# Conditioning weights in tiles of 1024 columns, one step a tile, placed behind consecutive weight units

## The chip, the cores and the metric

One core of one Trainium2 chip runs the whole layer. The metric is the device time in microseconds (us) of one execution; lower is better. The kernel before takes 1895.23 us (median of 3 runs, 1892.63 to 1897.20).

## The reference

One layer of a streaming-encoder trunk on 256 frames of width 2048, all in f32: a SwiGLU branch (hidden width 5632), a mixer branch (multi-head latent attention beside a forgetting attention) and a second SwiGLU branch. Each branch is modulated by vectors that come from the conditioning row `c`:

```
cond = silu(c)                                  # (1, 2048)
mod  = cond @ w_ada + b_ada                     # w_ada is 2048 x 18432
sh1, sc1, gt1, sh2, sc2, gt2, sh3, sc3, gt3 = split(mod, 9)
h = modulate(rmsnorm(x, g_pre), sh, sc)         # h * (1 + sc) + sh
y = rmsnorm(swiglu(h, w_gate, w_up, w_down), g_post)
x = x + 0.5 * gt * y                            # the mixer: x + gt2 * rmsnorm(mixer(h))
```

The change concerns only how `cond @ w_ada` is computed beside the large products. That product is one row by 151 MB of weights.

## The kernel before, in words

**The large products.** All weights stream through the core once. A weight unit ("W") is 256 rows by 512 columns, 512 KB, one DMA into a slot of `raw`. ScalarE rounds it to fp32r (`w_hi`, L566), VectorE takes the difference (`w_lo`, L925), and TensorE makes 12 products of it (L1459 to L1461: hi by hi, hi by lo, lo by hi, two row chunks, two frame tiles). In four blocks of the projection stage `win` (n = 2 to 5) the weights stand as the loaded operand and a unit is 24 products of 256 columns (L1508 to L1511).

**The conditioning product.** It doesn't go to TensorE but to VectorE: a tile ("A") of `w_ada` is multiplied by a column of `silu(c)` and added to `acc` (`ada_unit`). A tile holds, on each partition, 2 rows of 512 columns (512 KB), so it takes two dependent steps (L944) with a drain ahead of each. Eight tiles make a "quarter" of 512 columns; then a transpose (L950) and a reduction (L953) put the sums over 32 partitions into `part_sum`, and later TensorE finishes the sum over partitions (`sum_columns`, L1616) and VectorE adds the bias (`mod_columns`). The first 64 tiles' worth is done at the start by another path (`start_ada`, L965, steps of 1024 columns), which the change leaves alone.

**The order of the work.** It is written out in `make_plan`. Blocks follow each other: `pre` and `gu1` (gate and up of the first SwiGLU, 16 W a block, the first four blocks opened together), `down1` (4 blocks of 22 W), `win` (8 blocks of 8 W), `uq`, `ukv`, attention, `wo` (4 blocks of 8 W), `gu2`, `down2`. `pattern(n_w, ada_after)` says behind which W of a block an A stands. The same order holds on SP's queue (the DMAs), on ScalarE and on VectorE. 32 KB of each partition are a ring of 8 slots (`RING`) shared by W and A; `w_lo` is written over the W's own slot, and `w_hi` has 4 buffers (`HI_RING`). A load waits until the tile 8 places ahead of it in the order is done with: a W when TensorE has finished it (`w_used`), an A when VectorE has (`raw_used`). SP issues strictly in order.

VectorE also has work at fixed places of a block: in `gu` blocks `hidden` before W4 (L1103) and `lo_hid` before W7 (L1109), in `down` blocks the eviction of the block before at W4 (L1120), in `win` blocks many small ones (`before_unit`). Four groups of conditioning columns have to be complete at set places, the ends of `GROUPS`: quarters 12, 20, 24, 32 and 36. `RUNS` says which blocks run as a hardware loop.

Of the kernel before, what the change touches and what calls it, by code (L numbers as in the profile page):

```python
# [93 lines left out]
class Block:  # L94
# [17 lines left out]
    def r_of(self, u):  # L112
        return self.r + self.seq.index(("W", u))

    def quarter(self, u):
        return (self.a + u) // 8, (self.a + u) % 8


def make_plan():
    at = dict(r=0, w=0, a=0, g=0)  # L120
    pl = {}


    pl["pre"] = [Block(at, woven(WOVEN.count("W") * "W"), 3 * OPEN)]
    at["a"] += 2 * KD * DB // 2
    gu_ada = pattern(16, [4, 5, 7, 8, 10, 11, 13, 14])
    gu = pattern(16, [])

    gu_ada0 = pattern(16, list(range(8, 16)))
    pl["gu1"] = [Block(at, woven(text), 2) for text in ("WWAWAW", "WWAWAW", "WWAWWA", "WWAWAW")]  # L130
    pl["gu1"] += [Block(at, gu_ada, 2) for b in range(OPEN_FF, FB - 4)]
    gu_more = [u for u in range(16) if u % 4 != 3]
    pl["gu1"] += [Block(at, pattern(16, gu_more), 2) for b in range(4)]

    pl["down1"] = [Block(at, pattern(22, [u for u in range(2, 21) if u % 6 != 4] if n < DB - 1 else list(range(0, 16, 2))), 1) for n in range(DB)]
    win_ada = [[6, 7], [3, 5, 7], [1, 3, 5, 6, 7]] + 5 * [[1, 3, 4, 5, 6, 7]]
    pl["win"] = [Block(at, pattern(8, after), 1) for after in win_ada]
    pl["uq"] = [Block(at, pattern(2, []), 1) for _ in range(3)]
    pl["ukv"] = [Block(at, pattern(1, []), 1) for _ in range(4)]
    pl["wo"] = [Block(at, pattern(8, after), 1)  # L140
                for after in ([1, 2, 3, 4], [1, 3, 4, 5, 6, 7], [1, 3, 4, 5, 6, 7], [])]
    pl["gu2"] = [Block(at, gu_ada0 if b == 0 else gu_ada if b < 4 else gu, 2) for b in range(FB)]
    pl["down2"] = [Block(at, pattern(22, []), 1) for _ in range(DB)]
    assert at["a"] == 8 * N_MOD * DB
    order = [kind for blocks in sorted(pl.values(), key=lambda v: v[0].r) for b in blocks for kind, _ in b.seq]
    assert len(order) == at["r"]


    tp, owner = {}, []

    def fills(name, n, by):
        tp[name] = len(owner)
        owner.extend((by * n)[:n])

    for f in ("1", "2"):

        fills("mod" + f, 8 if f == "1" else 4, "a" if f == "1" else "va")
        fills("hid" + f, 2 * (FB - 1), "v")
        fills("gate" + f, 4, "a")
        fills("hidlast" + f, 2, "v")  # L160
        if f == "1":
            fills("modmix", 4, "va")
            fills("qa", 2, "v")
            fills("kv", 1, "v")
            fills("kpe", 1, "v")
            fills("qr", 2, "v")
            fills("pt", 2 * HEADS, "a")
            fills("gatemix", 4, "a")
    taken = [(o, owner[:n + 1].count(o)) for n, o in enumerate(owner)]
    return pl, tp, taken, order  # L170


def build(nc, A, const, out):
    pl, tp, taken, order = make_plan()
    ctx = ExitStack()
    with ctx:
# [22 lines left out]
        x = sb("x", [P, TT, D])  # L199
        y = sb("y", [P, TT, D])  # L200
        s = sb("s", [P, TT, NB])
        acc = sb("acc", [P, 2, NB])
        tmp = sb("tmp", [P, 2, NB])

        h_hi = sb("h_hi", [P, KD, SEQ], F32R)
# [2 lines left out]
        with ExitStack() as mix:  # L208
            def mx(name, shape, dt=F32):
                return mix.enter_context(nc.sbuf_tensor(name, shape, dt))  # L210
            qa_hi = mx("qa_hi", [P, Q_RANK // P, SEQ], F32R)
            qa_lo = mx("qa_lo", [P, Q_RANK // P, SEQ], F32R)
            ka_hi = mx("ka_hi", [P, KV_RANK // P, SEQ], F32R)
            ka_lo = mx("ka_lo", [P, KV_RANK // P, SEQ], F32R)
            fqk = mx("fqk", [P, 2 * HEADS, SEQ])
            fv = mx("fv", [P, TT, HEADS * P])
            v_mla = mx("v_mla", [P, TT, HEADS * DV])
            qnT = mx("qnT", [P, HEADS, SEQ])
            knT = mx("knT", [P, HEADS, SEQ])

            qrT = mx("qrT", [P, HEADS // 2, SEQ])
            krT = mx("krT", [P, 2, SEQ])
            sel = mx("sel", [P, HEADS, P])
            sel_b = mx("sel_b", [P, HEADS, P], BF16)
            lf = mx("lf", [P, TT, P])

            cumT = mx("cumT", [P, SEQ], BF16)
# [19 lines left out]
        newton = sb("newton", [P, TT])  # L247
        warm = sb("warm", [P, 1])
        rstd = sb("rstd", [P, TT])
        kpe = sb("kpe", [P, 2, TT, 2 * ROPE])  # L250
        forget = sb("forget", [P, KD, HEADS])
        fz = sb("fz", [P, 5, TT, HEADS])
        nbias = sb("nbias", [P, 2, TT])
# [110 lines left out]
        GATE = {"ffn1": 0, "mix": 1, "ffn2": 2}  # L364
        N_ATT = 2 * HEADS

        RUNS = {"gu1": ((OPEN_FF, FB - 4 - OPEN_FF), (FB - 4, 1), (FB - 3, 1), (FB - 2, 1), (FB - 1, 1)), "gu2": ((1, 1), (2, 2), (4, 1), (5, FB - 5))}

        def start_weight(w):

# [45 lines left out]

        @block.sync
        def _(sp):
            ada = A["w_ada"].rearrange("(p j) n -> p j n", j=KD)

            def load(r, src, n=NB, i=0, per=0, per_w=0):

# [6 lines left out]
                        sp.wait_ge(raw_used, plus(before + 1, i, per))  # L429
                sp.dma_start(raw[:, r % RING, :, 0:n], src).then_inc(raw_landed[r % RING], 16)  # L430

            def stream(b, unit, i=0, per=0, per_w=0, per_q=0):

                for n, (kind, u) in enumerate(b.seq):
                    if kind == "W":
                        src, cols = unit(u)
                        load(b.r + n, src, cols, i, per, per_w)
                    else:
                        q, j = b.quarter(u)
                        c0, j = plus(q, i, per_q) * NB, 2 * j  # L440
                        load(b.r + n, ada[:, j:j + 2, bass.ds(c0, NB)], NB, i, per, per_w)

            def unit_of(w, cols, at):
                v = w.rearrange("(k p) n -> p k n", p=P)
# [40 lines left out]
            for f, gu, down in (("1", "gu1", "down1"), ("2", "gu2", "down2")):  # L485
# [6 lines left out]
                for start, count in RUNS[gu]:  # L492
                    b = pl[gu][start]
                    if count == 1:
                        stream(b, gate_up(wg, wu, start))
                        continue
                    with sp.Fori(0, count) as i:
                        stream(b, gate_up(wg, wu, i + start), i, len(b.seq), 16, int(b.na > 0))
                for n, b in enumerate(pl[down]):
                    stream(b, unit_of(wd, NB, n * NB))  # L500
                if f == "2":
# [415 lines left out]
        def _(dve):  # L917
# [7 lines left out]
                nc.vector.tensor_tensor(w_lo[:, r % RING, :, 0:n], raw[:, r % RING, :, 0:n],  # L925
                                        w_hi[:, w % HI_RING, :, 0:n], ALU.subtract).then_inc(raw_used, 1)

            def ada_unit(b, n, a, i=0, per=0):


                r, (q, j0) = b.r + n, b.quarter(a)
                if j0:
                    dve.drain()  # L933
                dve.wait_ge(raw_landed[r % RING], landed(r, i, per))
                for k in range(2):
                    j = 2 * j0 + k
                    into = acc[:, 0, :]
                    if k:
                        dve.drain()
                    if j == 0:  # L940
                        ins = nc.vector.tensor_scalar(into, raw[:, r % RING, k, :], c_col[:, 1, j:j + 1],
                                                      None, ALU.mult)
                    else:
                        ins = nc.vector.scalar_tensor_tensor(into, raw[:, r % RING, k, :], c_col[:, 1, j:j + 1],  # L944
                                                             into, ALU.mult, ALU.add)
                ins.then_inc(raw_used, 1)
                if j0 == 7:
                    first, _, base = next(g for g in GROUPS if g[0] <= q < g[1])
                    dve.drain()
                    nc.vector.transpose(acc[:, 1, :], acc[:, 0, :])  # L950
                    dve.drain()
                    at = bass.ds(plus((base + q - first) * 4 * DB, i, 4 * DB if per else 0), 4 * DB)
                    nc.vector.tensor_reduce(part_sum[:, at], acc[:, 1, :].rearrange("p (b j) -> p b j", j=32), AX_X,  # L953
                                            ALU.add).then_inc(part_ready, 1)

            def start_ada(n):

# [10 lines left out]
            def run(b, tasks=None, i=0, per=0, per_w=0, start=0, stop=None, n=NB, before=None):  # L968
# [3 lines left out]
                for at in range(a, z):  # L972
                    kind, u = b.seq[at]
                    if kind == "A":
                        ada_unit(b, at, u, i, per)
                        continue
                    if before is not None:
                        before(u)
# [238 lines left out]
            for f, gu, down in (("1", "gu1", "down1"), ("2", "gu2", "down2")):  # L1217
# [29 lines left out]
                for n, b in enumerate(pl[down]):  # L1247
                    def last_down(n=n):
                        if n:
                            evac_y(pl[down][n - 1], k_y, n - 1, gate_ffn, fills[n - 1])  # L1250

                    def sums(n=n):
                        mod_columns(n // 2 + 1)
                    run(b, {4: last_down, 16: sums} if f == "1" and n in (1, 3) else {4: last_down}, start=2 if n == 0 else 0)
                if f == "2":
                    branch_end(pl[down][-1], k_y, gate_ffn, fills[-1])
                    break
# [192 lines left out]
        def _(pe):  # L1450
# [232 lines left out]
            for f, gu, down in (("1", "gu1", "down1"), ("2", "gu2", "down2")):  # L1683
# [25 lines left out]
                for n, b in enumerate(pl[down]):  # L1709
                    bank_free(b.g)  # L1710
                    for u in range(18 if n == DB - 1 else 22):
                        if n == 0 and u == 20:
                            pe.wait_ge(t_taken[who], count)
                        if f == "1" and n in (1, 3) and u == 6:
                            sum_columns(n // 2 + 1)
                        unit(b, u, hid_hi, hid_lo, 2 * u, b.g, u == 0, u == 21)
                    if n == DB - 1:
                        skewed_units(b, hid_hi, hid_lo, lambda u: 2 * u)
                if f == "2":
# [208 lines left out]
```

## Time and profile before

| | us |
|---|---|
| median of 3 runs | 1895.23 |
| lowest and highest | 1892.63, 1897.20 |
| the profiled execution, its own time | 1891.84 |
| its span, first to last instruction | 1890.1 |
| TensorE busy in it | 1850.8 (98%) |
| VectorE busy | 1359.9 (72%) |
| ScalarE busy | 895.2 (47%) |

The granted TensorE clock was 0.998 over the span. A busy time counts from the start of an instruction to its modelled end, and the products of TensorE overlap: two starts in a row are closer together than one product is long.

### The profile page before, as it was taken

The page shows a single profiled execution, that of the slowest core. Times are in us where ns is not written, and L with a number is a line of the kernel's source. Part 1 is how long each engine was busy: PE and PEld are TensorE (multiplying, and loading weights), DVE is VectorE, ACT ScalarE, POOL GpSimd, SP SyncE. Part 2 cuts the span into 40 slices and gives each one's busy share as a digit, 9 for nine tenths or more (in the row PEclk, how much of TensorE's full clock was granted, in tenths as well). Part 3 has the DMA queues.
Part 4 walks back from the last instruction along what each step waited for, and adds up shares of the span by engine and source line. Part 5 has one row for each costly group of instructions (what it writes and reads, how often), then busy time and mean ns, then how long its engine had stood idle before and what let it go on. Part 6 is the DMA issues. An engine that isn't in the chain of part 4 may idle for free.

```text
span 1890.1 us, 24649 instructions
## 1 busy us (share of the span) xinstructions
PE 1850.8 (98%) x9016; PEld 1557.5 (82%) x9016; DVE 1359.9 (72%) x1618; ACT 895.2 (47%) x1145; POOL 0.2 (0%) x4
## 2 busy tenths in 40 slices
PE   6999999999999999999999999999999999999998
PEld 6888888888888878899988788888888888888886
DVE  5998877889888888789786778878445445444444
ACT  4677644444444434654446446444444444434443
POOL 0000000000000000000000000000000000000000
PEclk9999999999999999999999999999999999999999
DMA  9998788999989998578992685888666666555553
GB/s 374 407 399 275 238 278 286 322 326 332 325 291 331 333 317 305 180 257 277 322 311 69 208 282 180 307 288 282 211 189 189 189 189 188 178 191 195 194 192 131
DMA packets 265052, 488.47 MB, mean 258 GB/s; under 512 B 21638, under 2 KB 32252, under 8 KB 264700
## 3 DMA queue, kind: packets, MB, share of 16 engines
q1 hardware_dynamic: 264080, 486.67, 76.7%
q8 instruction: 59, 0.97, 0.2%
q10 hardware_dynamic: 876, 0.53, 0.1%
q14 instruction: 37, 0.30, 0.1%
HBM read 485.04 MB, written 2.10 MB: 258 GB/s over the span
## 4 chain that ended last, share of the span: by engine, by line
PE 81%; DVE 8%; DMA 5%; DVEq 3%; ACT 2%; issue 1%; ACTq 0%; SPq 0%
PE pair L1459 25%; PE pair L1461 25%; PE pair L1460 25%; DVE acc L944 2%; DVE w_lo L925 2%; PE tps L1542 2%; DMA raw<-in_w_down 1%; DVEq L933 1%; DVE start_acc L965 1%; DMA raw<-in_w_in 1%; DMA start_raw<-in_w_ada 1%; ACT w_hi L566 1%; DVEq L964 1%; DMA raw<-in_w_up 1%; DMA raw<-in_w_gate 1%
## 5 line engine op out<-in xcount | busy, mean ns | idle before, releaser
L566 ACT ACTIVATE w_hi<-raw 128x1024 fp32r<-128x1024 f32 x634 | 667.9, 1056 | 883.1 <-PE pair L1461 417.4
L925 DVE TENSOR_TENSOR w_lo<-raw,w_hi 128x1024 fp32r<-128x1024 f32 x634 | 767.7, 1217 | 385.2 <-ACT w_hi L566 382.9
L1459 PE MATMUL pair<-w_hi,h_hi 128*128 128x512 f32 (+1 forms) x1656 | 645.8, 390 | 4.2 <-DVE w_lo L925 2.9
L1461 PE MATMUL pair<-w_hi,h_lo 128*128 128x512 f32 (+1 forms) x1656 | 642.3, 388 | 0.0
L1460 PE MATMUL pair<-w_lo,h_hi 128*128 128x512 f32 (+1 forms) x1656 | 641.9, 388 | 0.0
L1459 PEld LDWEIGHTS pair<-w_hi,h_hi 128*128 128x128 f32 x1656 | 310.9, 188 | 68.2 <-issue 2.9
L1461 PEld LDWEIGHTS pair<-w_hi,h_lo 128*128 128x128 f32 x1656 | 310.9, 188 | 63.9
L1460 PEld LDWEIGHTS pair<-w_lo,h_hi 128*128 128x128 f32 x1656 | 311.0, 188 | 61.9
L944 DVE SCALAR_TENSOR_TENSOR acc<-raw,c_col,acc 128x512 f32<-128x512 f32 x420 | 315.7, 752 | 47.8 <-DMA raw<-in_w_ada 12.7
L1459 PE MATMUL pair<-w_hi,hid_hi 128*128 128x512 f32 x704 | 275.6, 391 | 1.3 <-DVE w_lo L925 1.2
L1461 PE MATMUL pair<-w_hi,hid_lo 128*128 128x512 f32 x704 | 274.1, 389 | 0.0
L1460 PE MATMUL pair<-w_lo,hid_hi 128*128 128x512 f32 x704 | 274.0, 389 | 0.0
L1459 PEld LDWEIGHTS pair<-w_hi,hid_hi 128*128 128x128 f32 x704 | 132.1, 188 | 32.8 <-DVE w_lo L925 5.8
L1461 PEld LDWEIGHTS pair<-w_hi,hid_lo 128*128 128x128 f32 x704 | 132.1, 188 | 27.7
L1460 PEld LDWEIGHTS pair<-w_lo,hid_hi 128*128 128x128 f32 x704 | 132.2, 188 | 26.9
L965 DVE SCALAR_TENSOR_TENSOR start_acc<-start_raw,c_col,start_acc 128x1024 f32<-128x1024 f32 x55 | 70.7, 1285 | 14.7 <-DMA start_raw<-in_w_ada 9.7
L1508 PE MATMUL pair<-h_hi,w_hi 128*128 128x256 f32 x256 | 73.1, 286 | 4.5 <-DVE w_lo L925 4.5
L1510 PE MATMUL pair<-h_lo,w_hi 128*128 128x256 f32 x256 | 72.4, 283 | 0.0
L1511 PE MATMUL pair<-h_hi,w_lo 128*128 128x256 f32 x256 | 72.4, 283 | 0.0
L1508 PEld LDWEIGHTS pair<-h_hi,w_hi 128*128 128x128 f32 x256 | 49.1, 192 | 5.5 <-DVE w_lo L925 2.9
L1510 PEld LDWEIGHTS pair<-h_lo,w_hi 128*128 128x128 f32 x256 | 49.1, 192 | 0.0
L1511 PEld LDWEIGHTS pair<-h_hi,w_lo 128*128 128x128 f32 x256 | 49.1, 192 | 0.0
(211 smaller groups left out, 872.9 us busy)
## 6 DMA issues: line engine op xcount, KB each, us to landing
raw<-in_w_ada SPq DMA_DIRECT2D x224, 512.0 KB, 4.6
raw<-in_w_gate SPq DMA_DIRECT2D x176, 512.0 KB, 4.3
raw<-in_w_up SPq DMA_DIRECT2D x176, 512.0 KB, 4.0
raw<-in_w_down SPq DMA_DIRECT2D x176, 512.0 KB, 4.0
start_raw<-in_w_ada SPq DMA_DIRECT2D x64, 512.0 KB, 9.4
raw<-in_w_in SPq DMA_DIRECT2D x56, 512.0 KB, 4.8
raw<-in_w_o SPq DMA_DIRECT2D x32, 512.0 KB, 4.7
raw<-in_w_uq SPq DMA_DIRECT2D x12, 256.0 KB, 4.3
```

The lines of the kernel that those rows point to most:

```text
L566: nc.scalar.activation(w_hi[:, w % HI_RING, :, 0:n], raw[:, r % RING, :, 0:n], ACT.Copy).then_inc(hi_ready, 1)
L925: nc.vector.tensor_tensor(w_lo[:, r % RING, :, 0:n], raw[:, r % RING, :, 0:n], w_hi[:, w % HI_RING, :, 0:n], ALU.subtract).then_inc(raw_us ...
L933: dve.drain()
L944: ins = nc.vector.scalar_tensor_tensor(into, raw[:, r % RING, k, :], c_col[:, 1, j:j + 1], into, ALU.mult, ALU.add)
L965: ins = nc.vector.scalar_tensor_tensor(total, tile, c_col[:, 1, j:j + 1], total, ALU.mult, ALU.add)
L1459: nc.tensor.matmul(o, hi, wh, start=first and kk == 0, stop=False, skip_group_check=added)
L1460: nc.tensor.matmul(o, hi, wl, start=False, stop=False, skip_group_check=added)
L1461: ins = nc.tensor.matmul(o, lo, wh, start=False, stop=last and kk == 1, skip_group_check=added)
L1508: nc.tensor.matmul(o, wh, hi, start=first and kk == 0 and c % 2 == 0, stop=False, skip_group_check=True)
L1510: nc.tensor.matmul(o, wh, lo, start=False, stop=False, skip_group_check=True)
L1511: ins = nc.tensor.matmul(o, wl, hi, start=False, stop=last and kk == 1, skip_group_check=True)
L1542: ins = nc.tensor.transpose(tps[0:rows, n % 2, k * P:(k + 1) * P], src, ident)
```

## The change

What it does:

- An A tile now holds, on each partition, one row of 1024 columns (two quarters, a "half"), and takes one step; 16 tiles make a half. `acc` has three parts: two for the sums and one for the transpose.
- At the end of a half the first quarter is transposed and reduced at once (`row_sums`), the second ahead of the first step of the next half, or at once too where a group ends there (after quarters 11, 19, 23, 31, 35).
- The number of A tiles (224 here) and of W units in each block stays; their places change in `gu1` blocks 7 to 10 (12 A, behind u = 4 to 15, before behind each u with u % 4 != 3) and in `down1` (16 A behind u = 4 to 19, before behind 16 of u = 2 to 20; in the last block 8 A behind u = 4 to 11, before behind every second u).
- Blocks with A tiles no longer run as loops (`RUNS`): `gu1` 4 to 6 and `gu2` 2 and 3 are written out.
- `sum_columns` and `mod_columns` in `down1` stand at the end of blocks 0 and 2, and behind the eviction in blocks 1 and 3.
- `kpe` lies in another part of the memory.

```diff
-    def quarter(self, u):
-        return (self.a + u) // 8, (self.a + u) % 8
+    def half(self, u):
+
+        return divmod(self.a + u, KD)
...
-    gu_more = [u for u in range(16) if u % 4 != 3]
+    gu_more = [4, 5, 6, 7, 8, 9, 10, 11, 12, 13, 14, 15]
...
-    pl["down1"] = [Block(at, pattern(22, [u for u in range(2, 21) if u % 6 != 4] if n < DB - 1 else list(range(0, 16, 2))), 1) for n in range(DB)]
+    pl["down1"] = [Block(at, pattern(22, list(range(4, 20 if n < DB - 1 else 12))), 1) for n in range(DB)]
...
-        RUNS = {"gu1": ((OPEN_FF, FB - 4 - OPEN_FF), (FB - 4, 1), (FB - 3, 1), (FB - 2, 1), (FB - 1, 1)), "gu2": ((1, 1), (2, 2), (4, 1), (5, FB - 5))}
+        RUNS = {"gu1": [(b, 1) for b in range(OPEN_FF, FB)], "gu2": [(b, 1) for b in range(1, 5)] + [(5, FB - 5)]}
...
-            ada = A["w_ada"].rearrange("(p j) n -> p j n", j=KD)
+            ada = A["w_ada"].rearrange("(p j) (q n) -> p j q n", j=KD, n=NB)
...
-                        q, j = b.quarter(u)
-                        c0, j = plus(q, i, per_q) * NB, 2 * j
-                        load(b.r + n, ada[:, j:j + 2, bass.ds(c0, NB)], NB, i, per, per_w)
+                        half, j = b.half(u)
+                        load(b.r + n, ada[:, j, 2 * half:2 * half + 2, :])
...
+            def ada_unit(b, n, a):
+
+                r, (half, j) = b.r + n, b.half(a)
+                dve.wait_ge(raw_landed[r % RING], landed(r))
+                into = acc[:, 0:2, :]
+                if j == 0:
+                    if not any(2 * half == first for first, _, _ in GROUPS):
+                        row_sums(2 * half - 1)
+                    ins = nc.vector.tensor_scalar(into, raw[:, r % RING], c_col[:, 1, 0:1], None, ALU.mult)
+                else:
                     dve.drain()
...
+                    ins = nc.vector.scalar_tensor_tensor(into, raw[:, r % RING], c_col[:, 1, j:j + 1], into,
+                                                         ALU.mult, ALU.add)
                 ins.then_inc(raw_used, 1)
...
+                if j == KD - 1:
+                    row_sums(2 * half)
+                    if any(2 * half + 2 == end for _, end, _ in GROUPS):
+                        row_sums(2 * half + 1)
+
+            def row_sums(q):
+
+                first, _, base = next(g for g in GROUPS if g[0] <= q < g[1])
+                at = 4 * DB * (base + q - first)
+                dve.drain()
+                nc.vector.transpose(acc[:, 2, :], acc[:, q % 2, :])
+                dve.drain()
+                nc.vector.tensor_reduce(part_sum[:, at:at + 4 * DB], acc[:, 2, :].rearrange("p (b j) -> p b j", j=32),
+                                        AX_X, ALU.add).then_inc(part_ready, 1)
...
-                        if f == "1" and n in (1, 3) and u == 6:
-                            sum_columns(n // 2 + 1)
                         unit(b, u, hid_hi, hid_lo, 2 * u, b.g, u == 0, u == 21)
+                    if f == "1" and n in (0, 2):
+                        sum_columns(n // 2 + 1)
```

## Rows read from the trace of the kernel before

**Rows 1.** The page, part 1: busy us, share of the span, instructions.
```profile
PE 1850.8 (98%) x9016; PEld 1557.5 (82%) x9016; DVE 1359.9 (72%) x1618; ACT 895.2 (47%) x1145; POOL 0.2 (0%) x4
```
**Rows 2.** The chain of waits, 560 to 724 and at 740: start, length, what.
```profile
571.82 5.92 DMA raw<-in_w_down
...
616.20 0.82 PE mps L1616 x8
...
680.28 6.27 DMA raw<-in_w_down
...
740.00 0.80 PE mps L1616 x8
```
**Rows 3.** Timeline of TensorE at four stalls: start, length, idle before and its releaser.
```profile
216.14 1.09 PE L1542 MATMUL tps<-cst,s 128*128 128x128 f32 x8 [1.13 <-DVE s L1103]
...
688.95 0.50 PE L1459 MATMUL pair<-w_hi,hid_hi 128*128 128x512 f32 x1 [0.30 <-DVE w_lo L925]
689.28 0.39 PE L1460 MATMUL pair<-w_lo,hid_hi 128*128 128x512 f32 x1
...
856.27 0.39 PE L1508 MATMUL pair<-h_hi,w_hi 128*128 128x256 f32 x1 [1.30 <-DVE w_lo L925]
...
1193.36 0.47 PE L1459 MATMUL pair<-w_hi,h_hi 128*128 128x512 f32 x1 [0.69 <-DVE w_lo L925]
```
**Rows 4.** TensorE's waits, 800 to 978: us in total, times, longest.
```profile
PE pair L1508 <- DVE w_lo L925: 4.5, 5, 1.3
PE pair L1459 <- DVE w_lo L925: 0.9, 1, 0.9
```
**Rows 5.** VectorE's groups over the span: busy us, mean ns of one.
```profile
L944 DVE SCALAR_TENSOR_TENSOR acc<-raw,c_col,acc 128x512 f32<-128x512 f32 x420 | 315.7, 752 | 47.8 <-DMA raw<-in_w_ada 12.7 <-issue 3.4
L965 DVE SCALAR_TENSOR_TENSOR start_acc<-start_raw,c_col,start_acc 128x1024 f32<-128x1024 f32 x55 | 70.7, 1285 | 14.7 <-DMA start_raw<-in_w_ada 9.7 <-issue 0.5
L962 DVE TENSOR_SCALAR start_acc<-start_raw,c_col 128x1024 f32<-128x1024 f32 x4 | 3.0, 749 | 5.1 <-ACT c_col L717 5.1
```
**Rows 6.** Timeline of VectorE, 943 to 951, a stretch without idle time.
```profile
943.40 1.57 DVE L944 SCALAR_TENSOR_TENSOR acc<-raw,c_col,acc 128x512 f32<-128x512 f32 x2
944.89 1.22 DVE L925 TENSOR_TENSOR w_lo<-raw,w_hi 128x1024 fp32r<-128x1024 f32 x1
946.20 1.57 DVE L944 SCALAR_TENSOR_TENSOR acc<-raw,c_col,acc 128x512 f32<-128x512 f32 x2
947.87 0.71 DVE L950 STREAM_TRANSPOSE acc<-acc 128x512 f32<-128x512 f32 x1
948.65 0.69 DVE L953 TENSOR_REDUCE part_sum<-acc 128x16 f32<-128x512 f32 x1
949.26 1.22 DVE L925 TENSOR_TENSOR w_lo<-raw,w_hi 128x1024 fp32r<-128x1024 f32 x1
```
**Rows 7.** SP's queue, 1173 to 1185: the DMAs of `gu2` block 0's last units.
```profile
1173.66 0.37 SPq L430 DMA_DIRECT2D raw<-in_w_up  x1
1174.07 0.47 SPq L430 DMA_DIRECT2D raw<-in_w_ada  x1
1176.38 0.37 SPq L430 DMA_DIRECT2D raw<-in_w_up  x1
...
1184.54 5.81 SPq L430 DMA_DIRECT2D raw<-in_w_gate  x5
```
**Rows 8.** ScalarE in the same stretch: start, length, idle before and its releaser.
```profile
1177.34 1.06 ACT L566 ACTIVATE w_hi<-raw 128x1024 fp32r<-128x1024 f32 x1 [1.94 <-DMA raw<-in_w_up]
...
1190.18 1.06 ACT L566 ACTIVATE w_hi<-raw 128x1024 fp32r<-128x1024 f32 x1 [3.26 <-DMA raw<-in_w_gate]
```
**Rows 9.** DMA, median us from issue to landing, 541:724, then 1400:1600.
```profile
raw<-in_w_down SPq DMA_DIRECT2D x65, 512.0 KB, 6.2
...
raw<-in_w_gate SPq DMA_DIRECT2D x39, 512.0 KB, 3.6
```
**Rows 10.** Window 95 to 140: PE, PEld, DVE, ACT, POOL busy us (instructions), PEclk, DMA share, GB/s.
```profile
95.00:140.00 45.00, 45.00 (x208) 37.48 (x207) 41.08 (x39) 36.16 (x54) 0.00 (x0) 1.00 1.05 400
```

More of the change, by code:

```diff
@@ L201, in build @@
         s = sb("s", [P, TT, NB])
-        acc = sb("acc", [P, 2, NB])
+        acc = sb("acc", [P, 3, NB])
         tmp = sb("tmp", [P, 2, NB])
@@ L223, in build @@
             sel = mx("sel", [P, HEADS, P])
+            kpe = mx("kpe", [P, 2, TT, 2 * ROPE])
             sel_b = mx("sel_b", [P, HEADS, P], BF16)
@@ L249, in build @@
         rstd = sb("rstd", [P, TT])
-        kpe = sb("kpe", [P, 2, TT, 2 * ROPE])
         forget = sb("forget", [P, KD, HEADS])
@@ L430, in load, with stream @@
                 sp.dma_start(raw[:, r % RING, :, 0:n], src).then_inc(raw_landed[r % RING], 16)
-            def stream(b, unit, i=0, per=0, per_w=0, per_q=0):
+            def stream(b, unit, i=0, per=0, per_w=0):
                 for n, (kind, u) in enumerate(b.seq):
@@ L497, in _ @@
                     with sp.Fori(0, count) as i:
-                        stream(b, gate_up(wg, wu, i + start), i, len(b.seq), 16, int(b.na > 0))
+                        stream(b, gate_up(wg, wu, i + start), i, len(b.seq), 16)
                 for n, b in enumerate(pl[down]):
@@ L926, in lo_unit @@
                                         w_hi[:, w % HI_RING, :, 0:n], ALU.subtract).then_inc(raw_used, 1)
-            def ada_unit(b, n, a, i=0, per=0):
-                r, (q, j0) = b.r + n, b.quarter(a)
-                if j0:
-                    dve.drain()
[L934 to L945, printed above, removed]
-                ins.then_inc(raw_used, 1)
[L947 to L954, printed above, removed]
@@ L974, in run @@
                     if kind == "A":
[L975 removed]
+                        ada_unit(b, at, u)
                         continue
@@ L1250, in last_down @@
                             evac_y(pl[down][n - 1], k_y, n - 1, gate_ffn, fills[n - 1])
-                    def sums(n=n):
-                        mod_columns(n // 2 + 1)
-                    run(b, {4: last_down, 16: sums} if f == "1" and n in (1, 3) else {4: last_down}, start=2 if n == 0 else 0)
+                            if f == "1" and n in (1, 3):
+                                mod_columns(n // 2 + 1)
+                    run(b, {4: last_down}, start=2 if n == 0 else 0)
                 if f == "2":
```

## The prediction

> **What bounds the kernel now.** The page's busy times come first: TensorE is busy 1850.8 of 1890.1 us [rows 1], so nothing the change does to VectorE or the DMAs can pay except where TensorE waits for them. TensorE's pitch is read off SP's queue: weight loads that wait for a finished unit are issued at 1173.66 and 1176.38, so a unit takes 2.72 us [rows 7]. I then looked for what lies between units in TensorE's waits, its timeline and the chain of waits. The waits that conditioning work has a hand in are these:
>
> - the end of the opening: TensorE waits 1.13 us for `s`, which VectorE makes after an A tile and a transpose and reduction [rows 3].
> - `win`: six waits for `w_lo`, 4.5 + 0.9 = 5.4 us [rows 4], the longest 1.30 at 856.27 [rows 3]. After a wait TensorE doesn't resume at pitch: at 688.95 the next product starts 0.33 us later [rows 3], where 12 products in 2.72 us are 0.23 apart, and more such starts follow. I put this at 0.3 us a wait, so `win` loses 5.4 + 6 x 0.3 = 7.2 us.
> - `down1`: the small sums stand at the same place (ahead of unit 6) of blocks 1 and 3, at 616.20 and 740.00 [rows 2]. Between them are 44 units (119.7 us) and one sum (0.8), but 123.8 us pass: 3.3 us are lost. Block 0 has one more such chain at 571.82 [rows 2]; with it I take 4.3 us.
> - the first unit of `gu2` block 1: 0.69 us at 1193.36 [rows 3], with its slow restart 1.0.
> - about 0.4 in `gu1` block 10 (estimate).
>
> With 1.13 + 0.6 for the opening that is 14.6 us in all: more than that the change cannot gain. The chain of waits names two kinds of cause. In `win` it is VectorE, in `down1` it is "DMA raw<-in_w_down" of 5.92 and 6.27 us, then ScalarE, then VectorE [rows 2].
>
> **What a tile costs VectorE.** From 943.40 to 946.20 one A tile and one weight unit take 2.80 us [rows 6], more than TensorE's 2.72, so VectorE falls behind wherever they alternate. A 512-column step is 0.752 us, a 1024-column one 1.285 [rows 5]; two steps stand as 1.57 to 1.58 [rows 6]. After the change the pair takes 2.80 - 1.58 + 1.285 = 2.51 us: VectorE gains 0.29 us a tile and is again faster than TensorE. The first tile of a half takes 0.749 [rows 5]. A transpose with its reduction delays the next unit from 1.49 after the step's start (943.40 to 944.89) to 3.06 (946.20 to 949.26), so it costs 1.57 [rows 6]; call it RS. There are 28 as before, but they now come in twos: both at once where a group ends, else one behind the sixteenth tile and one ahead of the next.
>
> **The slack of a weight load.** This is the part that speaks against the change. Where W and A strictly alternate, the 8 slots hold 4 W and 4 A, so the load of unit w waits until TensorE has finished unit w-4, and must be landed, rounded and subtracted in 3 x 2.72 = 8.16 us. ScalarE takes 1.06 [rows 8], VectorE 1.22 [rows 6], handing over some 0.1. So a load that takes L us to land is ready 5.78 - L ahead of TensorE, less 0.35 that I allow for TensorE's early weight loading (estimate). Where three A stand to four W, the slot eight places back mostly lies one unit earlier, and 2.72 us are added; the A tile is then issued ahead of the W, which costs the W about 0.9. The change gives up 1.85 us of slack in `gu1` 7 to 10 and in `down1`.
>
> What L is: 3.6 without A tiles, 6.2 as a median in `down1` [rows 9]. `gu2` block 0 already has eight strictly alternating tiles. Its W at 1173.66 is with ScalarE at 1177.34, so L = 3.66; the W at 1184.54, after eight pairs, at 1190.18, so L = 5.62 [rows 7, 8]. An alternating stretch asks for 1.049 MB in 2.72 us = 385 GB/s; the most that a long stretch shows is 400 [rows 10]. So a delay once made goes back by some 0.1 us a pair only.
>
> The Trainium skill's page "DMA: Bandwidth & Descriptors", section "Latency and other measured facts", puts the latency of the memory at 0.2 us on average and 2 us under high load. By it, L would rise by 1.8 to 5.46 throughout an alternating stretch. The 5.62 agrees, the 3.66 three tiles into the same stretch doesn't.
>
> **The sum.** Gains first.
>
> - Opening: RS is no longer behind that tile (the half ends eight tiles later) and two steps are shorter, 1.57 + 0.6 = 2.2 ahead of a wait of 1.13. It goes: -1.7.
> - `win`, with 40 tiles. Two of the RS just ahead of a wait (of quarters 26 and 28, at the end of block 3 and in block 6) move away; with 0.29 for each of the 5 to 6 tiles since VectorE last idled, the waits in block 3, at the start of block 4 and in block 6 go. Block 2 keeps its RS and gets the next one straight behind it: +1.57 - 0.29 x 3 - 0.57 leaves it as it is, 2.4. The wait at 909.32 is a slow DMA's; I keep 0.7 for it. 7.2 becomes 3.1: -4.1.
> - `gu2` block 1: RS between the last tile and W0 goes: -1.0.
>
> Then what alternation costs.
>
> - RS inside an alternating stretch. VectorE has 2.72 - 2.51 = 0.2 spare, so with one RS the next unit is ready 5.78 - 1.4 - L ahead, with two 2.93 - L. With the 0.35 the stall is L - 4.1 and L - 2.6. For `down1` I take L = 5.0, between 3.66 and 6.2 and nearer its own stage. Blocks 0 and 2 end their stretch with two RS: 2 x 2.4. Block 1 with one: 0.9. `gu1` block 9 has one behind W11 and one behind W12: 1.2. `wo` block 3 has one more ahead of W0, partly beside the small sum: 0.4. Together +7.3. What is queued behind an RS is every later `w_lo`; TensorE is who waits.
> - Loads that come late by themselves, W8 to W19 of three blocks in `down1`, 36 units. `gu2` block 0 shows 0 a unit, the waits of `down1` about 0.2 where a load had only this slack. I take 0.12, since a stall itself lets the DMAs catch up: +4.3. `gu1` 7 to 10, 35 units at 0.05: +1.8. Last block of `down1`: +0.2.
> - The old waits of `down1` and `gu1` 10 are replaced by these: -4.7.
>
> Net: -1.7 - 4.1 - 1.0 + 7.3 + 4.3 + 1.8 + 0.2 - 4.7 = +2.1 us.
>
> Costed at nothing: the small sums moved (same 0.8 us on TensorE each, their inputs ready, since the units behind the last A tile are behind it on VectorE too); `kpe`; the written-out loops (no wait stands at the loops' ends, and VectorE is several us ahead there; if code came late it would show as TensorE waiting for "issue"); SP issues the same number of DMAs. Whether rows of 4 KB move faster than two of 2 KB no row shows. They are 128 pieces in place of 256; for a half of the traffic I bound it by -0.1 us a tile and 0, and take 0.
>
> The profiled execution took 1891.84, 3.4 under the median. Made against its own time the sum gives 1893.9; on the median, 1895.2 + 2.1 = 1897.3.
>
> **The rivals.**
>
> A. *VectorE's relief wins.* The DMAs keep up in alternating stretches as in the first seven pairs of `gu2` block 0, L near 4.0. Then the RS cost 2 x 1.4 + 0.2 + 0.3 and late loads 1.0, together 4.3. Gains and old waits are 1.7 + 4.1 + 1.0 + 4.7 = 11.5, so the sum is -7.2: 1888. For it: VectorE is under TensorE's pitch everywhere, fewer and longer pieces, W ahead of A in each pair. Against it: `down1`'s 6.2 at a lower load than the change asks for.
>
> B. *The queue stays full.* L holds at 5.7 or more through each stretch, and every unit from W8 on comes late. The price is that of `down1`'s worst loads, 0.25 x 36 + 0.15 x 35 = 14.3, and the RS at L = 5.7 cost 2 x 3.1 + 1.6 + 1.9 + 0.6 = 10.3; less 11.5 that is +13: 1908. It decides from L above 5.4 as the stretch's mean. For it: rows 8's 5.62 and 385 against 400 GB/s. Against it: a stall delays the next issue, so both can't be paid in full. (The skill's page on DMAs, same section, is on B's side with the 5.46 worked out above.)
>
> C. *Nothing of this is seen*: VectorE's share was not what `win` waited for, and its loads are late too. Then `win` keeps its 7.2, and the sum is +6: 1901.
>
> **How the numbers follow.** A measurement tells this kernel from no change from about 0.2%, 3.8 us: below 1891.4 is faster, above 1899.0 slower. Forecast (1893 to 1901) 0.50, A 0.25, B 0.17, C 0.08. Faster: A's 0.23 and 0.01 of the rest. Slower: B, C and a fifth of the forecast, 0.35. The same: 0.41. The range runs from A's 1888 to short of B's 1908: 1888 to 1905.
>
> **What would show it.** `win`: TensorE's waits for `w_lo` at or under 3 us in place of 5.4, and steps of 1.28 us with a pair at 2.5. The opening: no wait for `s`. `down1`: waits ahead of W20 in blocks 0 and 2, 1 to 3 us each, behind two transposes and two reductions in a row; between the small sums nothing else over 1 us. Alternating loads issued at 2.72 us pitch, W then A, with L of 4.5 to 5.5. Wrong it would be if L stays under 4.2 there (A) or over 5.5 (B), or if TensorE waits for "issue".

## The result, and the profile after

The changed kernel takes 1899.78 us (median of 22 runs, 1892.85 to 1906.27) beside 1894.91 us for the kernel before (22 runs, 1890.10 to 1898.40): a ratio of 1.0025 [1.0016, 1.0035], 4.7 us slower. The forecast was 1897.3 with a range of 1888 to 1905. Its runs scatter over 13 us where those of the kernel before scatter over 8. The slower ones ran at a lower granted TensorE clock: two at 0.999 took 1894.3 us in the mean, ten at 0.997 took 1897.4, five at 0.996 took 1900.3 and five at 0.995 took 1904.0. Where that clock is lost is found below.

The profiled execution took 1902.35 us by its own time, 10.5 more than that of the kernel before. Its first weight unit ends 4.5 us later (at 45.7 against 41.2). The profiles of the experiments below, all alike up to there, fall into two sets too (44.9 to 45.6 and 41.4 to 41.9), so these 4.5 belong to the execution. From the start of `pre`'s units to the end the two traces differ by 5.9 us, and that is what has to be explained.

The page, parts 0 and 1, of the changed kernel (answers to [rows 1]):

```profile
span 1900.5 us, 23647 instructions
PE 1860.4 (98%) x9016; PEld 1568.4 (83%) x9016; DVE 1319.6 (69%) x1394; ACT 895.6 (47%) x1145; POOL 0.2 (0%) x4
```

VectorE lost 40.3 us of work in 224 instructions less, as the change says, and TensorE was busy 9.6 us longer with the same 9016 products. That is the first sign that some products ran more slowly; a part of it is the slow start.

**`down1`.** The chain of waits of the changed kernel from 586 to 609 and at 736 (start, length, what; answers to [rows 2]):

```profile
586.30 5.99 DMA raw<-in_w_down
592.31 1.07 ACT w_hi L566
593.41 1.23 DVE w_lo L925
594.72 1.28 DVE acc L939
596.10 0.71 DVE acc L953
596.89 0.69 DVE part_sum L955
597.67 0.71 DVE acc L953
598.45 0.69 DVE part_sum L955
599.14 1.14 DVE w_lo L925
600.42 0.76 PE pair L1460
608.99 0.82 PE mps L1617 x8
...
736.09 0.80 PE mps L1617 x8
```

This is the place that the prediction named: block 0's last A tile, then two transposes and reductions in a row, and behind them `w_lo` of W20. The small sums now stand at the ends of blocks 0 and 2. Between them lie 44 units (119.7 us) and one sum (0.8), and 127.1 us pass: 6.6 lost, where the like stretch before (from unit 6 of block 1 to unit 6 of block 3) lost 3.3.

TensorE's timeline at that place (start, length, idle before and its releaser; answers to [rows 3]):

```profile
597.31 0.39 PE L1462 MATMUL pair<-w_hi,hid_lo 128*128 128x512 f32 x1
600.42 0.76 PE L1460 MATMUL pair<-w_hi,hid_hi 128*128 128x512 f32 x1 [2.72 <-DVE w_lo L925]
600.98 0.63 PE L1461 MATMUL pair<-w_lo,hid_hi 128*128 128x512 f32 x1
601.41 0.63 PE L1462 MATMUL pair<-w_hi,hid_lo 128*128 128x512 f32 x1
...
606.77 0.40 PE L1460 MATMUL pair<-w_hi,hid_hi 128*128 128x512 f32 x1
607.01 0.39 PE L1461 MATMUL pair<-w_lo,hid_hi 128*128 128x512 f32 x1
```

A product before the wait takes 0.39 us and the next starts 0.23 later; after it they take 0.63 and start 0.43 apart, for 6.1 us, and then 0.39 again. The windows of the same trace tell why (stretch, length, busy us and instructions of PE, PEld, DVE, ACT and POOL, granted clock, DMA share, GB/s): around the wait, behind it, behind the wait in block 2, and in `win` block 2.

```profile
597.00:600.00 3.00, 0.70 (x4) 0.24 (x2) 2.83 (x4) 1.60 (x3) 0.00 (x0) 0.95 1.02 384
602.00:604.00 2.00, 2.00 (x7) 1.52 (x6) 1.68 (x2) 0.00 (x0) 0.00 (x0) 0.50 0.76 305
730.00:732.00 2.00, 2.00 (x6) 1.54 (x5) 2.00 (x2) 0.00 (x0) 0.00 (x0) 0.50 0.86 339
870.00:872.00 2.00, 2.00 (x11) 2.00 (x11) 2.00 (x3) 1.06 (x1) 0.00 (x0) 0.50 0.66 266
```

The granted clock is 0.50, the lower of the two levels (1.2 instead of 2.4 GHz), after waits of 2.72, 2.44 and 2.0 us. The stretches last 6.8, 3.4 and 3.4 us. The first began 0.7 us before TensorE resumed, so products ran in 6.1 us of it; half of the time with products is lost: 3.1 + 1.7 + 1.7 = 6.5 us. The profile before has no such stretch between the opening and the last 8 us, where every one of these profiles has one.

**`win`, `wo` and the steps.** TensorE's waits (us in total, times, longest), first over the whole span, then for 812 to 990, which is `win` (answers to [rows 4]):

```profile
PE pair L1460 <- DVE w_lo L925: 8.3, 9, 2.7
...
PE mps L1617 <- DVE part_sum L955: 1.5, 1, 1.5
...
PE pair L1509 <- DVE w_lo L925: 2.0, 1, 2.0
```

`win` has one wait of 2.0 us in place of six that made 5.4. It stands where two transposes and reductions have one unit between them, as VectorE's timeline of that place shows:

```profile
860.28 0.71 DVE L953 STREAM_TRANSPOSE acc<-acc 128x512 f32<-128x512 f32 x1
861.07 0.69 DVE L955 TENSOR_REDUCE part_sum<-acc 128x16 f32<-128x512 f32 x1
862.27 1.22 DVE L925 TENSOR_TENSOR w_lo<-raw,w_hi 128x1024 fp32r<-128x1024 f32 x1
863.58 0.71 DVE L953 STREAM_TRANSPOSE acc<-acc 128x512 f32<-128x512 f32 x1
864.37 0.69 DVE L955 TENSOR_REDUCE part_sum<-acc 128x16 f32<-128x512 f32 x1
```

A new wait stands in `wo` block 3, ahead of a small sum; and the group of the new steps (busy us, mean ns of one; idle time before them and what ended it; answers to [rows 5]) has the predicted 1285 ns. TensorE's row first, then VectorE's group:

```profile
1124.99 1.09 PE L1617 MATMUL mps<-part_sum,gather 128*128 128x32 f32 x8 [1.50 <-DVE part_sum L955]
...
L939 DVE SCALAR_TENSOR_TENSOR acc<-raw,c_col,acc 128x1024 f32<-128x1024 f32 x210 | 269.8, 1285 | 29.7 <-DMA raw<-in_w_ada 12.7
```

Block by block, from the times at which units end, less 2.72 us for each unit (my working from both traces), against the prediction's terms, its old waits put with the block that they belong to:

| | predicted | measured | half clock in it |
|---|---|---|---|
| opening | -1.7 | -1.7 | 0 |
| `gu1` 7 to 10 | +2.6 | +0.7 | 0 |
| `down1` | +5.9 | +9.6 | 4.8 |
| `win` | -4.1 | -2.7 | 1.7 |
| `wo` 3 | +0.4 | +2.1 | 0 |
| `gu2` 1 | -1.0 | -1.0 | 0 |
| all else | 0 | -1.1 | 0 |
| sum | +2.1 | +5.9 | 6.5 |

### The profile page after: what moved, and what is told of

The parts are those of the page before. It is cut to its first block, busy times and chain, and to the rows that moved or that the text cites. A ratio compares the mean times of both kernels' runs of the same rounds, so it can differ in the third digit from the quotient of the medians.

```text
span 1900.5 us, 23647 instructions
## 1 busy us (share of the span) xinstructions
PE 1860.4 (98%) x9016; PEld 1568.4 (83%) x9016; DVE 1319.6 (69%) x1394; ACT 895.6 (47%) x1145; POOL 0.2 (0%) x4
## 4 chain that ended last, share of the span: by engine, by line
PE 90%; DVE 4%; DMA 3%; ACT 1%; DVEq 1%; issue 0%; ACTq 0%; SPq 0%
PE pair L1460 27%; PE pair L1461 27%; PE pair L1462 27%; PE tps L1543 2%; PE pair L1509 2%; PE pair L1512 2%; PE pair L1511 2%; DVE w_lo L925 1%; DMA raw<-in_w_down 1%; DMA start_raw<-in_w_ada 1%; PE mps L1581 1%; DVE acc L939 1%; ACT w_hi L566 1%; DVE x L1141 1%; DVE acc L953 0%
## 5 line engine op out<-in xcount | busy, mean ns | idle before, releaser
L939 DVE SCALAR_TENSOR_TENSOR acc<-raw,c_col,acc 128x1024 f32<-128x1024 f32 x210 | 269.8, 1285 | 29.7 <-DMA raw<-in_w_ada 12.7
L967 DVE SCALAR_TENSOR_TENSOR start_acc<-start_raw,c_col,start_acc 128x1024 f32<-128x1024 f32 x55 | 70.7, 1285 | 15.5 <-DMA start_raw<-in_w_ada 10.5
```

The lines of the kernel that those rows point to most:

```text
L939: ins = nc.vector.scalar_tensor_tensor(into, raw[:, r % RING], c_col[:, 1, j:j + 1], into, ALU.mult, ALU.add)
L967: ins = nc.vector.scalar_tensor_tensor(total, tile, c_col[:, 1, j:j + 1], total, ALU.mult, ALU.add)
```

## The experiments

All times are medians, and a ratio is to the kernel before measured beside it on the same chip, with its 95% interval. The experiments were measured in three groups, and the kernel before stood at 1894.05 us in the first (`after_again` to `wide_spread`), 1895.82 in the second (`sums_late2` to `best`) and 1893.76 in the third (`best_again`, `best_together`).

**The changed kernel again** (`after_again`), unedited, as the base for the others.

> The changed kernel itself, as the base for the others of this call. Expected 5 us over the kernel before (22 runs gave 1.0025). Theory 'sums': the loss is the two transposes and reductions in a row behind the last conditioning tile of down1 blocks 0 and 2 (waits of 2.72 and 2.44 us in its profile), and after waits of over 2 us TensorE runs for 3.4 to 6.8 us at half its clock. Theory 'loads': the loss is late weight loads in the alternating stretches. Both expect the same here; in the profile 'sums' expects waits of over 2 us ahead of unit 20 of blocks 0 and 2, with the granted clock at 0.5 behind some of them.

Measured: 1898.08 us, 1.0024 [1.0010, 1.0038]. Its profile has the same three waits (2.70, 2.21, 2.02 us), but half clock after the first only, for 3.4 us. So the waits are the kernel's own, and what the clock makes of them changes from one execution to the next, by up to 5 us here.

**`down1`'s transposes and reductions later and one at a time** (`sums_late`): they wait until the A tiles of the block are through, and each then stands ahead of a weight unit that follows another weight unit. (The lines shown are without the branch for the first tile of a half.)

```diff
             def lo_unit(b, u, i=0, per=0, per_w=0, n=NB):
...
+                if pending and order[r - 1] == "W":
+                    row_sums(pending.pop(0))
...
                 if j == KD - 1:
-                    row_sums(2 * half)
-                    if any(2 * half + 2 == end for _, end, _ in GROUPS):
-                        row_sums(2 * half + 1)
+                    pending.extend((2 * half, 2 * half + 1))
+                    if not (b in pl["down1"]):
+                        row_sums(pending.pop(0))
+                        if any(2 * half + 2 == end for _, end, _ in GROUPS):
+                            row_sums(pending.pop(0))
```

> As the changed kernel, but in down1 the transposes and reductions of a finished half are done one at a time ahead of the next weight units that don't follow a conditioning tile (ahead of units 21 and 0, or 21 and 0 of the next block), in place of both at once ahead of unit 20. Places of tiles and loads unchanged. Theory 'sums': the waits ahead of unit 20 go (2.9 + 2.6 + 1.0 us in the profile) and with them the half clock behind two of them (3.4 + 1.7 us); 8 to 11 us less than the changed kernel, so 3 to 6 us under the kernel before. Theory 'loads': no change against the changed kernel, 5 us over before.

Measured: 1893.13 us, 0.9994 [0.9982, 1.0005]. The stalls at W20 are gone: blocks 1 and 2 lose 0.96 and 0.47 us. But my edit also put the second quarter that `gu1` block 10 leaves over ahead of the last `hidden`, and TensorE waited 2.02 us for `s` at 538.77, again followed by half clock; block 0 still lost 8.18. A repeat without that is below.

**TensorE kept busy** (`warm20`): the above left out, 20 transposes of a constant on TensorE ahead of W20 in blocks 0 and 2 of `down1`, in the time in which it would wait.

```diff
+                        if f == "1" and n in (0, 2) and u == 20:
+                            keep_warm(20)
                         unit(b, u, hid_hi, hid_lo, 2 * u, b.g, u == 0, u == 21)
```

> As the changed kernel, but TensorE does 20 transposes of the identity ahead of unit 20 of down1 blocks 0 and 2, that is in the time in which it would wait. The output is the same. If the half clock comes from TensorE's idle time of over 2 us, it stays at full clock there: 3 to 5 us less than the changed kernel (about as the kernel before), the waits cut by some 2 us and filled with the transposes. If the slow products behind the waits have another cause (VectorE or the DMAs on the memory), they stay and the time is that of the changed kernel, 5 us over before.

Measured: 1893.58 us, 1.0001 [0.9989, 1.0014], 4.4 us under `after_again` by the ratios. TensorE's timeline and a window behind it:

```profile
594.07 2.35 PE L1607 MATMUL mps<-cst 128*128 128x128 f32 x20
596.84 0.50 PE L1460 MATMUL pair<-w_hi,hid_hi 128*128 128x512 f32 x1 [0.43 <-DVE w_lo L925]
...
598.00:600.00 2.00, 2.00 (x11) 1.65 (x10) 2.00 (x2) 0.07 (x1) 0.00 (x0) 1.00 0.92 370
```

The unit starts no earlier in its chain than it would have, since `w_lo` is what it waits for (it is 2.77 us behind its pitch, 2.88 in the changed kernel); what differs is the clock, 1.00 in place of 0.50. The time without work costs what it did, and the half clock, which is what the filler takes away, is worth about 4 us of the median.

**Wide tiles in the old places** (`wide_spread`):

```diff
-    gu_more = [4, 5, 6, 7, 8, 9, 10, 11, 12, 13, 14, 15]
+    gu_more = [u for u in range(16) if u % 4 != 3]
-    pl["down1"] = [Block(at, pattern(22, list(range(4, 20 if n < DB - 1 else 12))), 1) for n in range(DB)]
+    pl["down1"] = [Block(at, pattern(22, [u for u in range(2, 21) if u % 6 != 4] if n < DB - 1 else list(range(0, 16, 2))), 1) for n in range(DB)]
```

> The changed kernel with the places of the kernel before (gu1 blocks 7 to 10 and down1): tiles of 1024 columns, spread. Theory 'sums': the two transposes and reductions in a row stay, now ahead of unit 21 of down1 blocks 0 and 2; the time is 2 to 4 us over the kernel before, little under the changed kernel. Theory 'loads': the spread order gives its slack back; the wide tiles' gains of some 7 us in the opening, win and gu2 are left: 4 to 7 us under the kernel before.

Measured: 1889.30 us, 0.9977 [0.9963, 0.9990]: 4.4 us faster than the kernel before, which is what theory 'loads' had expected. It doesn't decide for that theory, though: the old places give slack to a unit held up by VectorE as well as to one whose load is late. In `down1` the stalls at the transposes and reductions (two in a row, one, two in a row) are 0.81, 1.48 and 0.81 us, where the changed kernel has 2.9, 1.0 and 2.6.

**The late sums without the slip** (`sums_late2`):

```diff
-                    if not any(2 * half == first for first, _, _ in GROUPS):
+                    while late:
+                        row_sums(late.pop(0))
+                    if 2 * half - 1 in owed:
+                        owed.remove(2 * half - 1)
                         row_sums(2 * half - 1)
```

(`owed` holds the second quarter of a half that ends outside of `down1`, and it is done where the changed kernel does it.)

> As sums_late (both transposes and reductions of a half that ends in a down1 block are done one at a time ahead of later weight units), but the one left over from gu1 block 10 stays where the changed kernel has it. In sums_late it had slipped ahead of the last hidden() of gu1, where TensorE then waited 2.02 us and ran 3.4 us at half clock. Theory 'sums': that wait falls back to 0.3 to 0.6, so 3 us less than sums_late: 4 us under the kernel before. If the waits only move elsewhere: as sums_late, 0.9994 of before.

Measured: 1892.14 us, 0.9977 [0.9966, 0.9989] (against 1.0024 in the changed kernel). `down1` loses 4.72, 0.93, 1.54 and 0.97 us by block, 8.2 in all for 19.1. VectorE's timeline where block 0's stall was:

```profile
595.51 1.29 DVE L946 SCALAR_TENSOR_TENSOR acc<-raw,c_col,acc 128x1024 f32<-128x1024 f32 x1
596.71 1.22 DVE L929 TENSOR_TENSOR w_lo<-raw,w_hi 128x1024 fp32r<-128x1024 f32 x1
598.03 0.71 DVE L965 STREAM_TRANSPOSE acc<-acc 128x512 f32<-128x512 f32 x1
598.81 0.69 DVE L967 TENSOR_REDUCE part_sum<-acc 128x16 f32<-128x512 f32 x1
599.41 1.21 DVE L929 TENSOR_TENSOR w_lo<-raw,w_hi 128x1024 fp32r<-128x1024 f32 x1
```

W20's `w_lo` comes straight behind the last step, and one transpose and reduction follows it. The W and A tiles, their places and the transfers are those of the changed kernel; so its `down1` was held up mostly by VectorE's five transposes and reductions of 1.57 us each, four of which came in twos, and not by transfers.

**Two steps in a wide tile** (`two_steps`): `wide_spread` with 512 columns a step again, to part the step from the 4 KB rows of the transfer.

```diff
-                    ins = nc.vector.scalar_tensor_tensor(into, raw[:, r % RING], ...)
+                    for k in range(2):
+                        dve.drain()
+                        ins = nc.vector.scalar_tensor_tensor(acc[:, k, :], raw[:, r % RING, k, :], ...)
```

(The first tile of a half is worked in two steps in the same way.)

> wide_spread with each wide tile worked in two steps of 512 columns: VectorE's cost of a tile is that of the kernel before (1.58 us), the DMAs and places those of wide_spread. If the gain of wide_spread over the kernel before (4.7 us) comes from VectorE's 0.29 us a tile, the waits for w_lo in win return and the time is that of the kernel before or 2 to 4 us over it (the sums still come in twos). If it comes from the longer rows of the DMAs (4 KB for 2 KB), it stays 4 to 5 us under.

Measured: 1899.30 us, 1.0022 [1.0007, 1.0037], 8.5 us more than `wide_spread`'s ratio gives. VectorE's row, then the medians from issue to landing in `down1` for the changed kernel, and the row on `w_down` for `two_steps` (the kernel before: [rows 9]):

```profile
862.98 1.59 DVE L941 SCALAR_TENSOR_TENSOR acc<-raw,c_col,acc 128x512 f32<-128x512 f32 x2
```

```profile
raw<-in_w_down SPq DMA_DIRECT2D x63, 512.0 KB, 5.2
raw<-in_w_ada SPq DMA_DIRECT2D x46, 512.0 KB, 5.9
```

```profile
raw<-in_w_down SPq DMA_DIRECT2D x65, 512.0 KB, 6.1
```

With the old places a W takes 6.1 us with 4 KB rows beside it and 6.2 with 2 KB rows, and an A 5.4 and 5.6, so longer rows move hardly faster, and the time with them alone is over that of the kernel before. What the width gains is VectorE's 0.29 us a tile. The Trainium skill's page "VectorE: DVE Perf Modes", section "The TRN2 errata — SBUF-src ops pay a fixed extra latency per instruction", says that an instruction pays a fixed extra latency, a large tile once and small ones each; this case agrees, with 1.285 us for one step and 1.59 for two.

**Narrow tiles in the new places** (`narrow_together`): the kernel before with the changed kernel's `gu_more` and `down1` patterns, the reverse of `wide_spread`'s diff.

> The kernel before with the places of the changed one (behind consecutive units), narrow tiles with two steps, sums one at a time. Theory 'sums' with the lost slack: a pair costs VectorE 2.80 us against TensorE's 2.72, so it falls behind by 1.3 us over 16 pairs and each transpose and reduction inside (two a block) adds 1.6: waits of 1 to 2 us each in down1 and gu1 9 to 10, 4 to 9 us over the kernel before. Theory 'loads': late loads show whatever the step: W8 to W20 of each down1 block wait 0.1 to 0.3 us each, with times to landing over 5.5 us.

Measured: 1906.91 us, 1.0064 [1.0049, 1.0079], 12 us slower. VectorE and TensorE at the first of seven such places (TensorE's waits there are 1.33 to 1.41 us):

```profile
571.36 1.57 DVE L944 SCALAR_TENSOR_TENSOR acc<-raw,c_col,acc 128x512 f32<-128x512 f32 x2
573.02 0.71 DVE L950 STREAM_TRANSPOSE acc<-acc 128x512 f32<-128x512 f32 x1
573.81 0.69 DVE L953 TENSOR_REDUCE part_sum<-acc 128x16 f32<-128x512 f32 x1
574.41 1.21 DVE L925 TENSOR_TENSOR w_lo<-raw,w_hi 128x1024 fp32r<-128x1024 f32 x1
...
575.68 0.50 PE L1459 MATMUL pair<-w_hi,hid_hi 128*128 128x512 f32 x1 [1.33 <-DVE w_lo L925]
```

No wait reaches 2 us and the clock stays up; seven waits of 1.37 and their slow restarts (0.3 each) are 11.7 us. By the starts of the same units the two profiles differ by 1.8 us in `gu1` 7 to 10 and by 11.3 in `down1`, where smaller new waits and the old ones that went also count. With the two kernels this gives the change in four corners:

| | old places | new places |
|---|---|---|
| narrow, two steps | 1.0000 | 1.0064 |
| wide, one step | 0.9977 | 1.0025 |

**A better order** (`best`, then `best_again`, the same kernel measured again beside the next): wide tiles in the old places; transposes and reductions late wherever two W follow, but not in `gu1`'s last block; the small sums back in blocks 1 and 3; 12 A in `down1`'s last block, and fewer in `win` blocks 1 and 2 and in `wo` block 2, so that quarters end elsewhere.

```diff
-                    if b in pl["down1"]:
+                    if order[r + 1:r + 3] == ["W", "W"] and b is not pl["gu1"][-1]:
                         late.extend((2 * half, 2 * half + 1))
...
-    win_ada = [[6, 7], [3, 5, 7], [1, 3, 5, 6, 7]] + 5 * [[1, 3, 4, 5, 6, 7]]
+    win_ada = [[6, 7], [3, 7], [3, 7]] + 5 * [[1, 3, 4, 5, 6, 7]]
-                for after in ([1, 2, 3, 4], [1, 3, 4, 5, 6, 7], [1, 3, 4, 5, 6, 7], [])]
+                for after in ([1, 2, 3, 4], [1, 2, 3, 4, 5, 6, 7], [0, 1, 2, 3, 4], [])]
```

> Wide tiles, one step each, in the spread places of the kernel before, and every pair of transposes and reductions that stood in front of a stalled unit moved: where two weight units follow the last tile of a half, they go one at a time ahead of the units after those. The last down1 block takes 12 tiles in place of 8 and win 36 in place of 40, wo has 4, 7 and 5, so that halves end at such places. Theory 'sums': against wide_spread the stalls ahead of unit 21 of down1 (0.8, 1.5, 0.8), of unit 7 in win block 2 (2.3, and 1.7 of half clock) and of wo block 3 (1.0) go: 7 to 8 us less than wide_spread, 1882 to 1884, ratio to before 0.993 to 0.995. If these waits are the DMAs' and only change their place: as wide_spread, 0.9977.

> The kernel best once more, as the base for best_together on the same chip: 0.995 of before.

Measured: 1885.44 us, 0.9952 [0.9937, 0.9966], and 1883.54, 0.9945 [0.9932, 0.9959]: 9 to 10 us faster than the kernel before, 14 to 15 faster than the changed one, and by the ratios 5 us under `wide_spread`, where 7 to 8 were expected. The page of `best`, and its waits for `w_lo` over the span:

```profile
span 1879.2 us, 23647 instructions
PE 1847.4 (98%) x9016; PEld 1558.3 (83%) x9016; DVE 1318.2 (70%) x1394; ACT 895.1 (48%) x1145; POOL 0.2 (0%) x4
...
PE pair L1473 <- DVE w_lo L929: 2.4, 6, 1.0
```

No wait for `w_lo` is over 1.0 us where the changed kernel's longest was 2.7, and the clock never halves behind one. TensorE's busy time is 13.0 us less with the same products, a part of which is that this execution had the fast start. Which of `best`'s edits brings how much wasn't taken apart, but for one:

**The better order in the new places** (`best_together`): `best` with `gu_more = [4, ..., 15]` and `down1` behind u = 4 to 19 (u = 4 to 15 in the last block).

> best with the places of the changed kernel (12 tiles behind units 4 to 15 in gu1 7 to 10, 16 behind 4 to 19 in down1, 12 behind 4 to 15 in its last block), the transposes and reductions of down1 still late. What the places cost by themselves, with the sums out of the way. From the profile of sums_late2: 1.2 to 1.4 us in gu1 block 9, where a half ends inside the stretch, 0.3 in the hand-over to down1, 1 to 2 us of single late loads: 3 us over best, 0.9965 to 0.9970 of before. Theory 'loads' with its full price (0.12 us a unit in down1, 0.05 in gu1): 6 us over best, 0.998.

Measured: 1884.76 us, 0.9946 [0.9932, 0.9959]. TensorE's waits from 541 to 745, all of `down1`:

```profile
PE pair L1473 <- DVE w_lo L929: 0.7, 1, 0.7
```

Sixteen strictly alternating pairs in a row, the load slack given up by 1.85 us, and 0.7 us of waits in that stretch, a single one behind a load that took 6.4 us to land. The kernel is 1.2 us over `best_again` by the medians and 0.2 by the ratios, of five runs each and with intervals of 2.6 us either way. In the profiles its `gu1` 7 to 10 and `down1` take 1.5 us more than in `best` and 2.1 more than in `best_again`. So the places cost some 1 to 2 us by themselves once the transposes and reductions are out of the way; the expected 3 are not ruled out, the 6 of theory 'loads' are. (Its profile is longer by more, mostly for a wait of 1.81 us and half clock in `win`, which the other two don't show.)

## Why the prediction was right, and where it was off

The time, the sign and most of the places were right; one whole cause was missing, and an overpriced term covered it.

- *Opening, `gu2` block 1, one step of 1285 ns:* as forecast, -1.7, -1.0 and 1285.
- *`win`, -4.1:* -4.4 without the half clock. The one wait left is where the text kept one, two transposes and reductions around one unit; rival C, with all of `win`'s 7.2 us still there, falls.
- *A double transpose and reduction at L = 5.0 costs 2.4:* TensorE waited 2.72 and 2.44 us for W20. (From the text's own terms, 5.78 - 3.14 + 0.2, the two leave 2.84 - L and not 2.93 - L, which makes the stall 2.5.) A single one, forecast at 0.9 in block 1: a wait of 0.68, and 0.98 lost with the slow restart. `gu1` block 9, forecast 1.2: +1.16. L in the alternating stretches was mostly 4.7 to 5.5 in `down1` (4.1 to 6.2 in all), which is neither A's 4.0 nor B's 5.7, and 3.6 to 4.9 in `gu1`, which is near A's. `narrow_together` and `sums_late2` show this to be most of the cost of the new places; `wide_spread` shows that the old places take the most of it away too.
- *Loads that come late by themselves, +6.3 in three terms: mis-sized.* The changed kernel shows some 2 us of them in `down1` and none in `gu1`; `best_together`, with the same places in the first three blocks, shows 1.7. Those are real: its one wait in `down1`, 0.66 us at 707.50, stands behind a load that took 6.4 us to land, and VectorE had been idle for 1.4 us before that unit. But they are single loads and not 0.12 us at every unit. I had taken the 0.12 from waits in the old `down1` that the profile put down to the DMA. A load is in that chain because the chain runs back through it; that isn't yet that it would decide if the transpose and reduction behind it were gone. This was rival B's mechanism too.
- *`wo` block 3, +0.4: mis-sized, +2.05.* The text had the transpose and reduction beside the small sum. But the sum reads what they make: TensorE waited 1.50 us for `part_sum` and then its units were late.
- *The clock: missing.* The text let TensorE resume 0.3 us late after any wait. That holds for the seven waits of up to 1.41 us in `narrow_together`; behind the three longest ones the clock was at half, which cost 6.5 us in the profiled execution. `warm20` takes it away in `down1` and gives 4.4 us back. The sum without it, with all terms at their measured size, is -0.6. That is no difference that can be told, and `warm20` at 1.0001 bears it out: the half clock is as much as the change is slower by.
- *At nothing:* the small sums in `down1` and the written-out loops cost nothing that shows, as forecast. One item was missed: the second quarter that `gu1` block 10 leaves over now comes ahead of its last `hidden`, and the wait for `s` behind it rose from 0.29 to 0.63. The new waits of 2.02 in `sums_late` show how near that is to a large one.

The forecast of +2.4 us on medians (1897.3 from 1894.9) met +4.7 because 4.3 too many for late loads stood beside 4.4 (6.5 in the profiled execution) too few for the clock, 1.6 for `wo` and some small ones. Being in the range was in part luck.

Open is why the slow start comes and goes. The trace shows only what it is: in the slow case products take the length of the half clock up to 43 us (sixteen filler transposes 3.62 us in place of 1.92), in the fast case up to 30 us, although the clock row reads 1.00 there in both. Open is also which of `best`'s edits in `win` and `wo` carries its gain.

## What to carry to other kernels

When tiles are made larger, the work at the end of each tile comes less often and in larger lumps; price each lump against the slack at its place, and spread it over the following units before moving anything else. Five such pieces of VectorE's work, moved by a unit or two, were worth 9 us here. The old placement, which gives every unit more slack, was worth the same 9 us with the lumps left in (`wide_spread`), but only 1 to 2 once they were spread.

A wait of TensorE isn't priced by its length alone: ask whether it is long enough that the products behind it run at the lower clock, and break up the longest waits first. Where runs scatter more than their neighbour's, compare the granted clock of the slow ones with that of the fast ones, and look for such a wait if it is lower. It isn't the only cause of scatter: the ten runs of `best` scatter over 12.5 us with clocks of 0.998 and 0.999.

## What the runs showed of the hardware

Over the profiles of all these kernels I found 13 waits of TensorE of 1.99 to 2.72 us in the middle of dense work, and 11 of them were followed by a granted clock of 0.50 for 3.4 or 6.8 us. Of some 60 waits of 0.9 to 1.8 us four were: 1.81 us in `win` of `best_together`, and 1.45, 1.10 and 0.92 us in `wo` of `sums_late`, `two_steps` and `sums_late2`. The last three stand ahead of the small sum, whose eight products of 32 columns take 1.1 us, and there the clock fell 1.9 to 2.2 us after TensorE had resumed. The same wait of the same kernel was followed by the half clock in one execution (2.44 and 2.03 in `after`) and not in the next (2.21 and 2.02 in `after_again`). Each such stretch costs half of the time that its products take, 1.7 or 3.1 us, on top of the wait. The Trainium skill's page "TensorE: Matmul & The Clock Gate", section "HAM oscillation — how this bites in real kernels", describes this of waits for DMA, longer ones than these, with the products behind each running at the lower clock; here waits for VectorE did it, and the 20 filler transposes of `warm20` kept it away.

An alternating stretch of W and A takes 5.2 us from issue to landing in the median for W and 5.9 for A, where the spread order has 6.2 and 5.6 in the kernel before and 6.0 and 5.4 with wide tiles (`wide_spread`): the sum hardly moves, and the tile that is issued first in the pair lands faster.
